# Two unused scratch tensors are taken out of the on-chip memory layout of a hybrid transformer kernel

## The reference

```python
h = h + swa_sink_attention(rms_norm(h, a_norm[j]), ...)        # 16 heads, 4 kv heads, window 128
h = h + swiglu(rms_norm(h, f_norm[j]), f_w_gate[j], f_w_up[j], f_w_down[j])
h = h + gated_deltanet(rms_norm(h, b_norm[j]), ...)            # 8 heads of 128, chunks of 64
h = h + moe_swiglu(rms_norm(h, m_norm[j]), m_w_router[j], m_w_gate[j], m_w_up[j], m_w_down[j])
return rms_norm(h, final_norm)
# swiglu(h) = (silu(h @ w_gate) * (h @ w_up)) @ w_down
```

## The kernel before

| tensor | first byte | | tensor | first byte |
|---|---|---|---|---|
| `pad_weights` | 1,152 | | `cst` | 133,120 |
| `w_high` | 2,048 | | `small_w` | 141,376 |
| `w_low` | 26,624 | | `pad_stages` | 143,680 |
| `w_raw` | 51,200 | | first tensor of each stage | 145,408 |
| `h` | 100,352 | | `qkv`, `qkT`, `prob` (attention) | 151,616, 176,192, 188,480 |
| `xs` | 108,544 | | `m_act`, `m_act_high` (experts) | 172,032, 174,080 |
| `x_high`, `x_low` | 116,736, 124,928 | | `fin`, `x_slots`, `y_slots` (experts) | 181,664, 198,048, 202,144 |

## Time and profile before

### The profile page before, as it was taken

The page is one execution under the profiler, slowest core; times in us unless marked ns, Lnnn a source line. Parts: engine busy times, 40 slices in busy tenths (PEclk is TensorE's granted clock), DMA queues, the critical chain, the costliest instruction groups (busy, mean ns, idle before and its releaser), DMA issues.

```text
span 1633.4 us, 22310 instructions
## 1 busy us (share of the span) xinstructions
PE 1530.7 (94%) x8225; PEld 1292.4 (79%) x8225; DVE 1214.0 (74%) x983; ACT 993.9 (61%) x931; POOL 94.0 (6%) x104
## 2 busy tenths in 40 slices
PE   5888999998989777899999999999999999999996
PEld 4777888877988676788888888888888888888884
DVE  5744555555576535788888888888888889888887
ACT  4444343434673434577777777777777777777773
POOL 0002000000122401100000000000000000000200
PEclk9789999998899878899999999999999999999998
DMA  9217755553332203699999999999999999999992
GB/s 341 92 39 272 285 187 181 193 191 105 104 129 79 80 1 104 244 377 376 389 380 364 398 375 374 392 377 375 390 367 383 382 381 376 383 380 360 417 409 86
DMA packets 92603, 453.96 MB, mean 278 GB/s; under 512 B 9872, under 2 KB 10256, under 8 KB 49552
## 3 DMA queue, kind: packets, MB, share of 16 engines
q1 hardware_dynamic: 83680, 430.83, 70.0%
q0 software_dynamic: 5616, 20.45, 3.1%
q10 hardware_dynamic: 3264, 2.08, 0.5%
HBM read 437.60 MB, written 15.73 MB: 278 GB/s over the span
## 4 chain that ended last, share of the span: by engine, by line
PE 90%; ACT 4%; DVE 4%; issue 1%; ACTq 1%; POOL 0%; DVEq 0%; POOLq 0%
PE PS L290 27%; PE PS L292 27%; PE PS L291 27%; PE PS L1348 1%; PE PS L917 1%; ACT w_high L278 1%; DVE w_low L282 1%; PE PS L991 1%; PE PS L1233 1%; ACT xs L562 1%; PE PS L967 1%; PE PS L1280 0%; PE PS L1224 0%; PE PS L980 0%; ACTq L549 0%
## 5 line engine op out<-in xcount | busy, mean ns | idle before, releaser
L282 DVE TENSOR_TENSOR w_low<-w_raw,w_high 128x2048 fp32r<-128x2048 f32 x408 | 936.1, 2297 | 238.5 <-ACT w_high L278 238.0
L278 ACT ACTIVATE w_high<-w_raw 128x2048 fp32r<-128x2048 f32 x408 | 781.3, 1918 | 361.1 <-PE PS L292 359.0
L290 PE MATMUL PS<-w_high,x_high 128*128 128x512 f32 x1264 | 501.5, 397 | 5.9 <-DVE x_low L1866 4.5
L292 PE MATMUL PS<-w_high,x_low 128*128 128x512 f32 x1264 | 494.1, 391 | 0.0
L291 PE MATMUL PS<-w_low,x_high 128*128 128x512 f32 x1264 | 493.6, 391 | 0.0
L290 PEld LDWEIGHTS PS<-w_high,x_high 128*128 128x128 f32 x1264 | 238.4, 189 | 56.1 <-DVE x_low L1866 4.6
L292 PEld LDWEIGHTS PS<-w_high,x_low 128*128 128x128 f32 x1264 | 238.1, 188 | 50.8
L291 PEld LDWEIGHTS PS<-w_low,x_high 128*128 128x128 f32 x1264 | 238.5, 189 | 47.4
L290 PE MATMUL PS<-w_high,m_act_high 128*128 128x512 f32 x448 | 175.0, 391 | 1.6 <-DVE m_act_low L1929 1.6
L292 PE MATMUL PS<-w_high,m_act_low 128*128 128x512 f32 x448 | 174.4, 389 | 0.0
L291 PE MATMUL PS<-w_low,m_act_high 128*128 128x512 f32 x448 | 174.4, 389 | 0.0
(11 more groups left out here) (272 smaller groups left out, 1282.8 us busy)
## 6 DMA issues: line engine op xcount, KB each, us to landing
w_raw<-in_m_w_blocks SPq DMA_DIRECT2D x336, 1024.0 KB, 7.0
w_raw<-in_b_w_in SPq DMA_DIRECT2D x16, 1024.0 KB, 5.4
w_raw<-in_f_w_gate SPq DMA_DIRECT2D x14, 1024.0 KB, 5.0
w_raw<-in_f_w_up SPq DMA_DIRECT2D x14, 1024.0 KB, 5.0
w_raw<-in_f_w_down SPq DMA_DIRECT2D x14, 1024.0 KB, 4.8
w_raw<-in_a_w_qkv SPq DMA_DIRECT2D x6, 1024.0 KB, 13.1
x_slots_dram<-zeros POOLq DMA_DIRECT2D x12, 512.0 KB, 7.5
w_raw<-in_a_w_o SPq DMA_DIRECT2D x4, 1024.0 KB, 6.9
```

The source lines that it names most:

```text
L278: nc.scalar.activation(WH[:, n % SPLIT, :], W[:, n % RAW, :], ACT.Copy).then_inc(hi_done, 1)
L282: nc.vector.tensor_tensor(WL[:, n % SPLIT, :], W[:, n % RAW, :], WH[:, n % SPLIT, :].bitcast(f32), ALU.subtract).then_inc(lo_done, 1)
L290: nc.tensor.matmul(o, sH, mH, start=first, stop=False)
L292: return nc.tensor.matmul(o, sL, mH, start=False, stop=last)
```

## The change

The two unused tensors are no longer allocated. Nothing else is edited: the instructions, their order, their waits and the sizes of all transfers are the same.

```diff
-        sb("pad_weights", [128, 224])
         WH = sb("w_high", [128, SPLIT, SUB], f32r)
         WL = sb("w_low", [128, SPLIT, SUB], f32r)
         W = sb("w_raw", [128, RAW, SUB])
...
         swL = sb("sw_low", [128, KD, 16 + E], f32r)
-        sb("pad_stages", [128, 432])
 
         with ExitStack() as c:
```

## The result

The changed kernel takes 1647.95 us in the median (1644.9 to 1652.8, 4 runs) against 1634.11 before (1632.4 to 1635.0): a ratio of 1.0087, with a 95% interval of 1.0062 to 1.0110. It is slower by 10 to 18 us where no change was forecast. All 23 executions of it that were taken lie between 1643.9 and 1657.9 us. The profiled execution has 1644.39 us, a span of 1642.8, which is 9.4 more than the span before.

A forecast was written before the change was run, and what follows sets the result against it. PE was taken to bound the kernel; 0 for TensorE, DVE and ACT, POOL and transfers left the profiled 1634.98 us, less 0.84 us to the median, so 1634.2 us, range 1630 to 1640 us.

The forecast's parts named there:

- What bounds the kernel: Whole kernel, mainly the experts: PE sets the pace, 94% busy and 90% of the chain; the DMA share of 0.99 is no limit.
- The step of 16.8 us: Experts: 72 matmuls at 0.2267 us, four transposes at 0.35 us and 0.13 us lost behind them make 16.8 us.
- VectorE, ScalarE, GpSimd, transfers: 0: Other engines and transfers: 0 us; bounds 1.3 us for DVE and ACT, 2 us for POOL, 2% for transfers.
- the transfer limit: Rival, experts: w_raw rows land late and PE waits; decides from 10% longer packets, 1679 us at 15%; chance 0.02.
- The small price for misaligned packets: Rival, transfers: up to 2% more a packet, hidden except around 1540 us, 1.0 us, 1635.2 us in all; chance 0.10.
- the bound of 2%: Transfers: the most that SBUF alignment could add to a packet, from POOL's two equal packet windows, 147 and 144 ns.
- TensorE: "I take 0": PE: the address move costs matmuls and transposes 0 us; bounds 5.1 us slower and 7.3 us faster.
- the 1 ns of two transposes: PE: transposes with differently aligned stationary operands take 272 against 271 ns, used to bound the 512-column matmuls.
- The forecast bound of 5.1 us: PE, two largest matmul groups: 5,136 matmuls at 1 ns each, 5.1 us at most, on the path.
- Slower matmuls: Rival, PE: moving fp32r operand pays for starting 128 bytes off a multiple of 256; 1639.3 us at 1 ns each; chance 0.05.
- Faster: Rival, experts: changed stage-to-weight-slot distance returns the 0.13 us a step lost behind transposes, 1626.9 us, or half, 1630.5; chance 0.06.
- The rule of the Trainium skill: Transfers into w_raw: rows starting off a multiple of 256 cost 260 beats in place of 256, 1.6%, 0.8 us in sum.

The follow-up runs named there:

- the two one-sided moves: Against the kernel before: only x_high and x_low moved by 320 bytes, 1660.68 us (1.0162); only w_high and w_low by 192, w_raw by 256, 1670.05 us (1.0201).

## Why the prediction was wrong

**What bounds the kernel** held. PE has work in all of every stretch of the experts, DVE, ACT and the transfers keep their slack, and so a loss of 6.6 ns a matmul comes out in full (24 of them are 0.16 us, and a step grew by 0.174). The step of 16.8 us was right.

**VectorE, ScalarE, GpSimd, transfers: 0** held. DVE's split stayed at 2,297 ns and landing from 800 to 1000 us at 7.0 us, and the transfer limit did not come. The small price for misaligned packets, to which I gave a chance of 0.10, is real, and as hidden as I had it. From 720 to 1500 us the median 8,192-byte packet takes 309 ns in all fourteen kernels. From 1540 to 1590 us, where the stream catches up, 94 to 99% of the packets still take at most 310 ns in the nine kernels with `w_raw` at a multiple of 256, and 23 to 43% in the five others (`w_raw` 128 bytes behind one, or 192). Of the packets between 300 and 335 ns the mean is 309.0 to 309.2 ns in the nine and 312.5 to 313.4 in the five, 1.1 to 1.4% more, inside the bound of 2%. Landing there goes from 8.2 us in the median and 10.8 at most to 8.5 and 11.8 in the changed kernel. It costs no time that can be seen: the kernel without `pad_weights` has these packets and a ratio of 1.0004.

**TensorE: "I take 0"** is the step that failed. The prediction named the hole, "No row shows a moving fp32r operand of 512 columns off its multiple", and then filled it with the 1 ns of two transposes, at 128 columns. What I compared there was each operand's own alignment. The transposes had in fact a distance off 256 as well (`x_slots` less `cst` is 64,928 bytes, 160 modulo 256) and showed nothing, and in the changed kernel those of `m_act` have one of 64 modulo 256 and still take 272 ns, so that they are no bound for the 512-column matmuls: those lose 6.6 ns. The forecast bound of 5.1 us assumed 1 ns on 5,136 matmuls; the runs show 6.6 ns on 1,680, the 1,344 down matmuls of the experts and the 336 of the dense stage, 11 us. Measured are 10 to 18 us; in the two profiles the 1.4 us at the end come on top. Only the 3,792 matmuls with `x` kept the pace that I forecast for all of them.

**"Slower matmuls"**, at 0.05, had the right engine and the wrong mechanism. It let the start 128 bytes off a multiple of 256 cost something. The kernel without `pad_weights` has just that and costs nothing. The whole loss comes with `pad_stages`, which moves no weight slot (1646.72 us, against 1647.95 with both gone).

**"Faster"** was the one place where I used that the distance between the stage tensors and the weight slots changes. I asked only whether the distance before could be a bad one. It was the good one: 172,032 bytes from `w_high` to `m_act_high`, 672 x 256, and the change made it 64 modulo 256. In the kernel before, every pair that PE reads in a 512-column matmul stood at a multiple of 256 apart. That could be read from the table of starts; that it mattered could not be read from the trace of before, which has no 512-column matmul of a pair off it. The honest bound would have been the pair never seen, with a chance well over 0.05.

**The rule of the Trainium skill** that I weighed ("DMA: Bandwidth & Descriptors", "How a descriptor splits into AXI transactions") would have made 0.8 us here, and was not the cause. The trace agrees with it in kind: the estimate of 1.6% from that page stands beside the 1.1 to 1.4% by which the packets between 1540 and 1590 us are longer where `w_raw` is off a multiple of 256. Another page bears on the cause: "SBUF — State Buffer", section "Who interferes with whom", gives PE two SBUF read ports, one for the moving operand and one for the weight load, and calls them independent. The trace does not agree in full: with instructions, data and clock the same, the pace goes from 0.2267 to 0.2333 us by the distance between the two operands alone. The measurement decides.

What stays open is what inside the chip the two reads share. That they collide is inferred from the two one-sided moves; no run shows the place. Nor do the runs tell whether the two belong to one matmul or to neighbours. The load of the next stationary operand runs beside a matmul (in the trace of before the load for L291 and the matmul of L290 both start at 1616.63 us), and nearly all neighbours here have the same distance. Distances were tried only in steps of 32 bytes, as the allocator gives them, and without 160.

## What to carry to other kernels

Where PE is the limit with fp32r matmuls of 512 columns, list the distance between the SBUF starts of each stationary and moving pair, and keep it a multiple of 256 bytes; here that is worth 3% of a matmul, and 192 bytes of padding buy it. Other types and widths were not tried, except transposes of 128 columns, which lost nothing. An edit that only moves addresses is no empty edit: it must be looked at by pairs of operands and not by each one's own alignment. A short operation's row is no bound for a long one of another shape.

## What the runs showed of the hardware that was not expected

- The pace of a 512-column fp32r matmul depends on the distance between its two operands modulo 256 bytes: 0.2267 us at 0, 0.2289 at 192, 0.2324 to 0.2342 at 32, 64, 96, 128 and 224. Absolute starts 64 bytes lower changed nothing (ratio 0.9998). The loss is there with ACT idle and no transfer under way (0.2333 against 0.2267 us).
- After a run of slow matmuls the pace does not recover at once. In the changed kernel the first six gate matmuls behind the down product of a plain step, of a pair at a good distance, are still at 0.228 to 0.236 us and only then at 0.2267, much as behind the transposes in the earlier trace rows.
- A transfer's packets of 8,192 bytes take 309 ns, and 1.1 to 1.4% more where their place in SBUF starts 128 or 192 bytes behind a multiple of 256; that shows in the stretch from 1540 to 1590 us, at 405 to 418 GB/s, and hardly elsewhere.
- Executions of one kernel spread by 10 to 14 us (1630.9 to 1640.6 for the kernel before in one set of 17, 1643.9 to 1657.9 for the changed one), and the stretches at half clock in attention differ between them: 0.76 against 0.84 between 64 and 130 us in the two profiles above.
